# The seam of branch merge and output projection in a hybrid decoder step: six output steps begun in the merge, weight loads and splits moved

## The reference, cut to what matters

```python
merged = sigmoid(h @ w_gate_a) * (branch_a @ w_proj_a) + sigmoid(h @ w_gate_b) * (branch_b @ w_proj_b)
y = merged @ w_out
x = x + rmsnorm(y, g1)
q = rmsnorm(x, g2) @ x_wq        # cross-attention queries
```

## Time and profile before

| | us |
|---|---|
| three runs | 2314.08, 2317.57, 2317.14 |
| median | 2317.14 |
| the profiled execution's own time | 2313.37 |
| its span | 2311.3 |
| TensorE busy in the span | 2185.7 (95%) |
| VectorE, ScalarE, GpSimd busy | 1277.4, 844.3, 594.1 |

### The profile page before, as it was taken

How to read it: one execution, slowest core, us unless ns; L and a number is a source line. 1 busy time by engine, 2 the same in 40 slices (tenths; PEclk the granted TensorE clock), 3 DMA queues, 4 the chain that set the end, 5 groups by cost and what they waited for, 6 DMA issues and landing times. The chain is left out here.

```text
span 2311.3 us, 42805 instructions
## 1 busy us (share of the span) xinstructions
PE 2185.7 (95%) x17107; PEld 2001.5 (87%) x17107; DVE 1277.4 (55%) x2350; ACT 844.3 (37%) x1712; POOL 594.1 (26%) x509
## 2 busy tenths in 40 slices
PE   9999998989888889999899999999899999999996
PEld 7799977865555579999899988898899999999996
DVE  2213345256665671132228145567899887876956
ACT  4221244216655660011225133554333333334343
POOL 0000025412232212112011300232244433445533
PEclk9999988879999999999999999998999999999998
DMA  4211097973453341111311156342223232264243
GB/s 151 100 49 48 29 156 235 305 277 117 137 165 110 125 141 42 60 44 53 112 56 37 37 190 239 114 139 84 88 96 114 73 119 89 103 236 162 90 137 127
DMA packets 133712, 276.33 MB, mean 120 GB/s; under 512 B 24626, under 2 KB 79571, under 8 KB 128332
## 3 DMA queue, kind: packets, MB, share of 16 engines
q1 hardware_dynamic: 110796, 232.32, 30.3%
q0 software_dynamic: 10368, 28.33, 3.7%
q10 hardware_dynamic: 12352, 12.96, 1.8%
HBM read 229.49 MB, written 48.26 MB: 120 GB/s over the span
## 5 line engine op out<-in xcount | busy, mean ns | idle before, releaser
L88 PE MATMUL psum<-merged_high,oq_half 128*128 128x352 f32 x768 | 189.6, 327 | 9.3 <-DVE oq_half L69 7.7
L88 PE MATMUL psum<-ff_t,ff_x_slots 128*128 128x264 f32 x1200 | 149.0, 284 | 0.0
L88 PEld LDWEIGHTS psum<-ff_t,ff_x_slots 128*128 128x128 f32 x1200 | 147.1, 188 | 0.1
L88 PEld LDWEIGHTS psum<-merged_high,oq_half 128*128 128x128 f32 x768 | 135.9, 191 | 9.9 <-DVE oq_half L69 8.0
L1655 POOL DMA_DIRECT2D na_kv<-in_pool x128 | 69.0, 539 | 226.8 <-PE psum L1859 156.4
L88 PE MATMUL psum<-x_half_high,mg_w_high 128*128 128x352 f32 x384 | 124.0, 323 | 1.9 <-ACT gated L2329 1.2
L88 PE MATMUL psum<-h_again_low,mg_w_high 128*128 128x352 f32 x384 | 123.1, 321 | 0.0
L88 PE MATMUL psum<-x_half_high,mg_w_low 128*128 128x352 f32 x384 | 123.0, 320 | 0.0
L1957 ACT ACTIVATE na_pt<-psum 128x512 f32<-128x512 f32 (+1 forms) x170 | 86.3, 543 | 89.5 <-PE psum L1832 81.0
L88 PE MATMUL psum<-ff_bslot,ff_x_slots 128*128 128x264 f32 x888 | 117.8, 286 | 0.7 <-DVE ff_z L4279 0.7
L88 PE MATMUL psum<-ff_t,ff_slot 128*128 128x264 f32 x840 | 106.8, 287 | 8.1 <-DVE ff_slot L69 6.4
(11 more groups left out here) (666 smaller groups left out, 5621.2 us busy)
## 6 DMA issues: line engine op xcount, KB each, us to landing
na_kv<-in_pool SPq DMA_DIRECT2D x128, 128.0 KB, 3.5
na_kv<-in_pool POOLq DMA_DIRECT2D x128, 128.0 KB, 4.2
ff_bslot_raw<-mid_ops SPq DMA_DIRECT2D x59, 264.0 KB, 3.2
mid_ops<-ff_bufs SPq DMA_DIRECT2D x11, 1056.0 KB, 3.9
mg_w<-in_w_merge SPq DMA_DIRECT2D x15, 768.0 KB, 4.4
ring<-in_f_wu SPq DMA_DIRECT2D x11, 1024.0 KB, 5.4
low<-in_f_wg SPq DMA_DIRECT2D x22, 512.0 KB, 4.6
first_pages<-in_pool SPq DMA_DIRECT2D x68, 128.0 KB, 5.4
```

The costliest lines, as they stand in the source:

```text
L88: ins = nc.tensor.matmul(out, w[a], x[b], start=first and n == 0, stop=last and n == 2)
```

## The change

- In the merge, behind the last unit's branch, TensorE runs output steps 0 to 5 (units 0 and 1, three groups each) over chunks 0 to 6: 126 matmuls into banks 0 to 5. The sums stay open. In the next stage these steps consist of chunk 7 alone, 18 matmuls.
- The high parts of output units 0 and 1 are made by ScalarE in the merge, between the last sigmoid and the copy of the last chunk; their low parts by VectorE ahead of the last unit's product.
- SP loads output units 2 and 3 in the merge, each when its slot is split. The next stage starts with splitting these; its loads of x are interleaved with those of units 4 to 6.
- The low parts of the second branch's operand are made behind unit 7's product, ahead of the cast for unit 9.
- Unit 0 of the merge: VectorE casts and splits the branch piece itself, then casts the gate piece; GpSimd splits the gate piece alone.

```diff
--- before.py
+++ after.py
@@ -2210,7 +2210,7 @@
...
-def merge(nc, A, h, high, low, hm, on, x_half, gated, dst_high, dst_low, over, ring, acc):
+def merge(nc, A, h, high, low, hm, on, x_half, gated, dst_high, dst_low, over, ring, out_half, acc):
@@ -2229,7 +2229,7 @@
...
         names = ("gate_ready", "branch_ready", "gate_drained", "branch_drained", "added", "parts_high", "parts", "w_high", "w_low",
-                 "x_high", "x_low", "b_high", "b_low", "ahead_loaded")
+                 "x_high", "x_low", "b_high", "b_low", "ahead_loaded", "first_high", "first_low", "out_high", "out_low")
         S = {n: sem(n) for n in names}
@@ -2257,13 +2257,15 @@
...
                         sp.dma_start(ring[:, j, :], A["w_out"][j]).then_inc(S["ahead_loaded"], 16)
-            sp.wait_ge(S["ahead_loaded"], 32)
+            for j in range(2):
+                sp.wait_ge(S["out_low"], j + 1)
+                sp.dma_start(ring[:, j, :], A["w_out"][2 + j]).then_inc(S["ahead_loaded"], 16)
+            sp.wait_ge(S["ahead_loaded"], 64)
...
             pool.wait_ge(S["w_high"], 1)
-            for c in (slice(GATE, UNIT), slice(0, GATE)):
-                low_part(nc.gpsimd, w_lo[:, 0, c], first_merge_unit(ring)[:, c], w_hi[:, 0, c]).then_inc(S["w_low"], 1)
+            low_part(nc.gpsimd, w_lo[:, 0, 0:GATE], first_merge_unit(ring)[:, 0:GATE], w_hi[:, 0, 0:GATE]).then_inc(S["w_low"], 1)
             for u in range(1, len(units)):
@@ -2271,7 +2273,7 @@
...
             def gates(u):
-                pe.wait_ge(S["w_low"], u + 2)
+                pe.wait_ge(S["w_low"], u + 1)
                 if u:
@@ -2286,7 +2288,10 @@
...
                 r = units[u][0]
-                pe.wait_ge(S["w_low"], u + 2 if u else 1)
+                if u:
+                    pe.wait_ge(S["w_low"], u + 1)
+                else:
+                    pe.wait_ge(S["first_low"], 1)
                 if r:
@@ -2306,6 +2311,18 @@
...
                 branch(u)
+            pe.wait_ge(S["gate_drained"], len(units))
+            pe.wait_ge(S["parts"], n_chunks - 1)
+            for j in range(2):
+                pe.wait_ge(S["out_low"], j + 1)
+                if j:
+                    pe.wait_ge(S["branch_drained"], len(units))
+                for g in range(NG):
+                    c = slice(g * GW, (g + 1) * GW)
+                    for k in range(n_chunks - 1):
+                        ks = slice(k * P, (k + 1) * P)
+                        split_product(nc, acc[:, NG * j + g, 0:GW], (out_half[:, j, 0, ks], out_half[:, j, 1, ks]),
+                                      (dst_high[:, k, c], dst_low[:, k, c]), k == 0, False)
@@ -2331,6 +2348,10 @@
...
                     nc.scalar.activation(in_groups(sg[:, :]), acc[:, 0:NG, 0:GW], ACT.Sigmoid).then_inc(S["gate_drained"], 1)
+                    if u == len(units) - 1:
+                        act.wait_ge(S["ahead_loaded"], 32)
+                        for j in range(2):
+                            nc.scalar.activation(out_half[:, j, 0, :], ring[:, j, :], ACT.Copy).then_inc(S["out_high"], 1)
                     act.wait_ge(S["added"], i + 1)
@@ -2342,7 +2363,11 @@
...
-            high_part(nc, w_hi[:, 0, :], first_merge_unit(ring)).then_inc(S["w_high"], 1)
+            b, a = slice(GATE, UNIT), slice(0, GATE)
+            high_part(nc, w_hi[:, 0, b], first_merge_unit(ring)[:, b]).then_inc(S["first_high"], 1)
+            ve.wait_ge(S["first_high"], 1)
+            low_part(nc.vector, w_lo[:, 0, b], first_merge_unit(ring)[:, b], w_hi[:, 0, b]).then_inc(S["first_low"], 1)
+            high_part(nc, w_hi[:, 0, a], first_merge_unit(ring)[:, a]).then_inc(S["w_high"], 1)
             for g in range(NG):
@@ -2350,10 +2375,10 @@
...
             for u, (r, i) in enumerate(units):
-                if u == n_chunks:
-                    for k in range(4):
-                        ve.wait_ge(S["b_high"], NG + k + 1)
-                        low_part(nc.vector, b_low[1][:, k, :], on[:, k, :], b_high[1][:, k, :]).then_inc(S["b_low"], 1)
+                if u == len(units) - 1:
+                    for j in range(2):
+                        ve.wait_ge(S["out_high"], j + 1)
+                        low_part(nc.vector, out_half[:, j, 1, :], ring[:, j, :], out_half[:, j, 0, :]).then_inc(S["out_low"], 1)
                 gate = gated[:, i, :] if r == 0 else sg[:, :]
@@ -2363,6 +2388,10 @@
...
                     low_part(nc.vector, dst_low[:, i, :], gate, dst_high[:, i, :]).then_inc(S["parts"], 1)
+                if u + 1 == n_chunks:
+                    for k in range(4):
+                        ve.wait_ge(S["b_high"], NG + k + 1)
+                        low_part(nc.vector, b_low[1][:, k, :], on[:, k, :], b_high[1][:, k, :]).then_inc(S["b_low"], 1)
                 if u + 2 < len(units):
@@ -2401,10 +2430,10 @@
...
         def wait_w_low(eng, u):
-            if u < 4:
-                eng.wait_ge(S["w_low"], u + 1)
-            else:
+            if u >= 4:
                 eng.wait_ge(S["w_low_pool"], u - 3)
+            elif u >= 2:
+                eng.wait_ge(S["w_low"], u - 1)
@@ -2427,7 +2456,8 @@
...
                 sp.dma_start(x[:, :, col(g)], A["x"][:, :, col(g)]).then_inc(x_loaded[g], 16)
-            for u in range(2, NU):
+                load_unit(4 + g)
+            for u in range(4 + NG, NU):
                 load_unit(u)
@@ -2447,7 +2477,7 @@
...
                     pe.wait_ge(S["low_ready"], KD * (g + 1))
-                for k in range(KD):
+                for k in range(KD - 1 if u < 2 else 0, KD):
                     ks = slice(k * P, (k + 1) * P)
@@ -2512,8 +2542,8 @@
...
                     act.wait_ge(S["steps_done"], last_step[u - 4] + 1)
-                if u >= 2:
-                    act.wait_ge(raw_loaded[u % 2], 16 * (u // 2))
+                if u >= 4:
+                    act.wait_ge(raw_loaded[u % 2], 16 * (u // 2 - 1))
                 nc.scalar.activation(half[:, u % 4, 0, :], ring[:, u % 2, :], ACT.Copy).then_inc(S["w_high"], 1)
@@ -2549,7 +2579,7 @@
...
-            for u in range(4):
+            for u in (2, 3):
                 weights_high(u)
@@ -2600,7 +2630,7 @@
...
             def weights_low(u):
-                pool.wait_ge(S["w_high"], u + 1)
+                pool.wait_ge(S["w_high"], u - 1)
                 low_part(nc.gpsimd, half[:, u % 4, 1, :], ring[:, u % 2, :], half[:, u % 4, 0, :]).then_inc(S["w_low_pool"], 1)
@@ -2614,7 +2644,7 @@
...
             def weights_low(u):
-                ve.wait_ge(S["w_high"], u + 1)
+                ve.wait_ge(S["w_high"], u - 1)
                 low_part(nc.vector, half[:, u % 4, 1, :], ring[:, u % 2, :], half[:, u % 4, 0, :]).then_inc(S["w_low"], 1)
@@ -4577,7 +4607,7 @@
...
         merge(nc, A, h, high, h_low, hm, zm, over("branch_half", "low", [P, KD, T]), tile_at("gated", [P, KD, T], m_at),
-              m_high, m_low, lambda name, at, shape: nc.alloc_sbuf_tensor_at(name, shape, F32R, offset=at), ring, psum)
+              m_high, m_low, lambda name, at, shape: nc.alloc_sbuf_tensor_at(name, shape, F32R, offset=at), ring, oq_half, psum)
         mem = tile_at("mem", [P, KD, MEM], nc.sbuf_base + 4 * (KD * MEM + 2 * D))
...
         mem_halves = (split_at("mem_high", [P, KD, MEM], high_at), split_at("mem_low", [P, KD, MEM], nc.sbuf_base + 4 * (KD * MEM + 2 * D)))
```

## The result

The changed kernel took 2298.01 us (median of six runs, 2292.41 to 2303.86) against 2313.84 us of the kernel before (six runs, 2306.79 to 2317.57). The ratio is 0.9938, 95% interval 0.9921 to 0.9955. That is 14.3 us at 2313.84 us, where the forecast had 12.0 us; the two medians themselves lie 15.8 us apart. Direction and mechanism held; the level and two sizes did not.

The account below looks back on a forecast made before the run. The prediction took TensorE, through its idle and lower-clock time, as the bound. Seam 9.5, middle 2.45 and start 0 sum to 12.0 us, scaled from the 2317.14 us median to 2305.1 us, range 2300.5 to 2310.5 us.

Parts of the forecast that it names:

- The seam: Between merge and next stage: six output steps begun early end at 1148.0 us against 1157.5 us, a gain of 9.5 us.
- The boundary's idle: TensorE's idle where the merge ends and the next stage starts: 0.5 us taken, bounds 0.33 and 0.88 us.
- Step seven: First output step after the six begun early: follows step six without a gap, costing nothing, slack 0.1 us.
- Case (d): At the seam, the first output unit's split comes late; only the middle is won, about 5 us, 2312 us; chance 0.06.
- Unit 4: Output unit 4's load behind one x group, in the next stage: lands in time, costs nothing, 2 us in hand.
- Rival (b): After the seam, unit 4 lands late and TensorE stalls 3.1 + 0.24 us, giving 2308.4 us; chance 0.08.
- The middle: Middle of the merge: TensorE's wait before the second branch goes, 2.21 us plus 0.24 us restart, 2.45 us.
- Later clock: Behind the seam: remaining stalls may or may not lower the clock; taken as 0, between -2.3 and +2.3 us.
- The start: Start of the merge, branch split moved to VectorE: taken as 0, between a 0.7 us gain and 1.1 us loss.
- That split is released by ScalarE and moves by nothing: Start of the merge: GpSimd's split of unit 1 stays in place, so an earlier TensorE start gains 0.
- Case (a): Start of the merge: GpSimd wins the shared port, holding VectorE's first split; loses 1.1 us, 2306.2 us; chance 0.18.
- Scaled to it: Whole kernel: the 12.0 us gain scaled from the profiled 2313.4 us to the runs' median 2317.14 us, giving 2305.1 us.

Follow-up runs that it names:

- after_again: The changed kernel run once more without an edit, against the kernel before: ratio 0.9936 (0.9923 to 0.9949).
- all_three: The changed kernel plus unit 0's sigmoid by column group, second group's sums a step later, output steps' end reordered; against the kernel before: ratio 0.9927.

## Why the prediction was wrong in its number and right in its mechanism

- **The seam, 9.5 us.** Right: 9.45 us in the first profile. The boundary's idle was 0.30 us where 0.5 us was taken, just under the lower bound of 0.33 us, so the agreement to 0.05 us is in part luck: a miss of 0.2 us was made up elsewhere in the stretch. Step seven followed without a gap. Case (d), the late split, did not occur: the splits ended at 1117.43 us, 1.4 us ahead of the product.
- **Unit 4, "cost nothing, 2 us in hand".** Right, with 3.6 us in hand (drained 10.7 us after the opening, asked for at 14.3 us). Rival (b) named the right mechanism, but its price was too small: with all of x ahead it costs 6.9 us and not 3.3 us, since the load took 14.2 us and the idle brings the clock down.
- **The middle, "2.21 + 0.24 = 2.45 us".** This term was mis-sized. In the profile that it was read from, the clock stayed at 1.00 behind the idle, and 2.54 us came out. In five of seven profiles with this idle the clock falls behind it, and the idle is worth 3.8 to 4.1 us. The part "Later clock" allowed for such a fall only behind the seam.
- **The start, "I take 0".** 0.5 us gained, within the bounds of -1.1 and 0.7 us. The step that failed here is "That split is released by ScalarE and moves by nothing. So an earlier start is swallowed". GpSimd's split of unit 1 begins at nearly the same place (11.73 us after the opening of the merge before, 11.85 us after the change), but its end moved from 15.92 to 15.42 us, and VectorE's split of h with it. Case (a) never occurred: VectorE had the port first in all eleven profiles with this edit.
- **Later clock, "I take 0".** Right for the first pair of profiles, where the clock fell behind the output steps before and after. In after_again it did not fall (seam stretch 204.5 us and not 206.1 us), which is inside the bounds.
- **"Scaled to it".** This is the step that put the time outside the range. The median of three runs, 2317.14 us, was taken as the level, and its own spread of 3.5 us as the scatter. With six runs the level is 2313.84 us, and in the later sets of runs, on four chips, it is 2307.9 to 2310.4 us. The two stretches that the change leaves alone scatter by 11.4 us ahead of the merge (828.45 to 839.81 us) and by 7.2 us from the memory stage on (972.4 to 979.6 us). At the six-run level the 12.0 us would have given 2301.8 us. The forecast of 2305.1 us was 7.1 us too long: 3.3 us are the level, 2.3 us the size of the gain, and the rest is that the medians lie 15.8 us apart where the ratio gives 14.3 us. A level 3.3 us lower would have put the range at 2297.2 to 2307.2 us, with the measured time in it; a gain 2.3 us larger alone would have put its lower end at 2298.2 us, still above 2298.01 us.
- **The sum.** Over the four profiles of the kernel before, merge to memory is 496.8 us (495.72, 497.31, 497.11, 497.24), over the two of the changed one 482.5 us. The difference of 14.3 us is that of the ratio (0.9938; 0.9936 in after_again). The 2.3 us above the forecast are 0.5 us at the start, about 1.1 us of clock in the middle, and 0.7 us at the seam and its later clock.
- **What stays open.** From the memory stage to the end the six profiles without an edit at the seam took 977.9 us on average (976.4 to 979.6), the twelve with one 975.1 us (972.4 to 977.4). The change has no instruction there. The difference lies in the clock: the time lost to it in the last stage (defined at the end) was 25.9 us on average in the six and 22.7 us in the twelve. Whether the clock fell otherwise by chance or behind a shorter merge was not settled; the intervals of the ratios (10.4 to 18.2 us) leave room for both. The runs without a profile lean to chance: over the ten kernels with an edit at the seam and a ratio, the ratios give 13.5 us on average and merge to memory alone 12.9 us, so little of the 2.8 us shows in them. Ahead of the merge the groups don't differ beyond their scatter (834.9 and 833.4 us), so the rival that those stages gain has no support.

## What to carry to other kernels

Where a stage ends in a chain of small operations on the last tile, begin the next stage's product over the tiles that are ready and leave the sum open in its bank. A moved part of 10 us hid a chain of 5 us as well as one of 20 us did. The moved part's weights must be split before it, and the next weights loaded as soon as their slots are free. Look then at what the next stage's queues put ahead of the drains: one weight load behind three large ones gave 6.9 of 9.5 us back in the one profile of it. And take the level and the scatter from the stretches that no edit touches; compare kernels by the stretch between two fixed events. Where the clock did not fall in it such a stretch repeated to 0.1 us (133.13 to 133.15 us from sigmoid 0 to 8), where whole times scatter by 10 us; where the clock can fall in it, it takes two values or more and wants several profiles.

## What the runs showed of the hardware

- The scatter of the last stage is the clock's. In 60 windows over the feed-forward stage, from its start to the end of the span, TensorE's idle is 39.0 to 39.8 us in all eighteen profiles, while the sum of window length times (1 - granted clock) goes from 18.8 to 26.9 us, and the stage from 841.8 to 849.5 us with it (correlation 0.95).
- A TensorE idle of 2.0 to 2.2 us left the clock at 1.00 in two profiles and was followed by a stretch at the lower level in five; the three idles of 0.86 to 1.44 us behind the output steps within some 25 us of each other did so in all but one of the profiles that kept them as they were. An idle must be priced by its chance of a fall, 1.3 to 1.6 us here, beside its length.
- At a stage's end where TensorE arrives last, it goes on after 0.30 us, nearly the same as where VectorE does (0.33 us in the earlier trace rows).
- VectorE, issuing its branch split 0.17 us ahead of GpSimd's, had the shared port first each time. The Trainium skill, page "SBUF — State Buffer", section "SBUF: two separate sides", says that whichever starts first holds it for the whole instruction; the trace agrees: GpSimd's split of 1024 columns took 3.68 us there, and 2.35 us in all_three with no split on VectorE beside it.
- GpSimd's split of unit 1, issued 11.7 to 12.1 us after the opening of the merge, near the end of a run of eight VectorE splits of h, ended 15.9 us after it in all seven profiles without the edit at the start, whether it took 3.87 or 4.20 us. With that edit VectorE's run ended 0.5 us earlier and so did GpSimd's split (15.4 to 15.6 us). It finished some 3.4 us behind VectorE's last split of the run, close to the 3.50 us that it takes by itself.
